# Two attention layers and a two-branch recurrence on one core: the gated branch's level products in column halves, the recurrence's quadrant products trimmed

## What is computed

```
b = jnp.cumsum(lf_c, axis=1)
diff = b[:, :, None] - b[:, None, :]
decay = jnp.where(causal, jnp.exp(jnp.where(causal, diff, 0.0)), 0.0)
att = jnp.einsum('btshd,bshd->btsh', q_c[:, :, None] * decay, k_c)
o_intra = jnp.einsum('btsh,bshv->bthv', att, i_c)
o_inter = jnp.einsum('bthd,bhdv->bthv', q_c * jnp.exp(b), S)
```

## Time and profile before

| | |
|---|---|
| median of 3 runs | 3076.45 us |
| the profiled execution | 3077.23 us, span 3075.4 us |
| TensorE busy | 2974.4 us (97%), 15930 records |
| weight loads | 2378.2 us |
| VectorE busy | 1698.2 us (55%) |
| ScalarE busy | 1210.0 us (39%) |
| mean granted clock of TensorE | 0.988 |

### The profile page before, as it was taken

The page is one execution under the profiler, slowest core; times in us unless marked ns, Lnnn a source line. Parts: engine busy times, 40 slices in busy tenths (PEclk is TensorE's granted clock), DMA queues, the critical chain, the costliest instruction groups (busy, mean ns, idle before and its releaser), DMA issues.

```text
span 3075.4 us, 40378 instructions
## 1 busy us (share of the span) xinstructions
PE 2974.4 (97%) x15930; PEld 2378.2 (77%) x15930; DVE 1698.2 (55%) x2880; ACT 1210.0 (39%) x2131; POOL 284.9 (9%) x517
## 2 busy tenths in 40 slices
PE   9999999999999999999999999999999999999897
PEld 7778787777878877777778877777777877867786
DVE  6554545555553336566553355657566666565647
ACT  5443443434332324344343333434444343434422
POOL 0110101010000000000000002202021020213001
PEclk9999999999999999999999999999999999999899
DMA  4222222222234321222234323223222231225334
GB/s 166 81 77 83 83 77 82 83 83 76 83 124 144 110 89 64 74 69 69 69 108 146 122 82 91 71 62 98 71 83 84 63 105 56 91 74 152 126 130 157
DMA packets 86011, 289.05 MB, mean 94 GB/s; under 512 B 12080, under 2 KB 12720, under 8 KB 85568
## 3 DMA queue, kind: packets, MB, share of 16 engines
q1 hardware_dynamic: 69696, 243.66, 23.4%
q0 software_dynamic: 16128, 42.81, 4.5%
HBM read 261.13 MB, written 25.17 MB: 93 GB/s over the span
## 4 chain that ended last, share of the span: by engine, by line
PE 82%; DVE 10%; ACT 4%; issue 3%; DMA 1%; POOL 0%; DVEq 0%; SPq 0%; ACTq 0%; POOLq 0%
PE bank L280 15%; PE bank L282 14%; PE bank L281 14%; PE bank L284 8%; PE bank L286 7%; PE bank L285 7%; PE bank L1420 2%; DVE mc_split L741 1%; ACT mc_split L573 1%; PE bank L337 1%; PE bank L317 1%; PE bank L1301 1%; PE bank L489 1%; PE bank L476 1%; PE bank L500 1%
## 5 line engine op out<-in xcount | busy, mean ns | idle before, releaser
L280 PE MATMUL bank<-ma_split,mc_split 128*128 128x512 f32 x2304 | 959.1, 416 | 12.1 <-DVE ma_split L895 7.2
L741 DVE TENSOR_TENSOR mc_split<-mc,mc_split 128x1024 fp32r<-128x1024 f32 x434 | 535.2, 1234 | 787.4 <-ACT mc_split L573 786.4
L282 PE MATMUL bank<-ma_split,mc_split 128*128 128x512 f32 x2304 | 906.8, 394 | 0.0
L281 PE MATMUL bank<-ma_split,mc_split 128*128 128x512 f32 x2304 | 904.0, 392 | 0.0
L573 ACT ACTIVATE mc_split<-mc 128x1024 fp32r<-128x1024 f32 x434 | 457.8, 1056 | 656.3 <-PE bank L284 349.4
L280 PEld LDWEIGHTS bank<-ma_split,mc_split 128*128 128x128 f32 x2304 | 437.2, 190 | 122.3 <-issue 48.6
L282 PEld LDWEIGHTS bank<-ma_split,mc_split 128*128 128x128 f32 x2304 | 435.5, 189 | 97.1
L281 PEld LDWEIGHTS bank<-ma_split,mc_split 128*128 128x128 f32 x2304 | 437.8, 190 | 79.0 <-issue 4.4
L284 PE MATMUL bank<-mc_split,ma_split 128*128 128x512 f32 x576 | 230.7, 401 | 5.0 <-DVE mb L1840 3.4
L286 PE MATMUL bank<-mc_split,ma_split 128*128 128x512 f32 x576 | 225.7, 392 | 0.0
L285 PE MATMUL bank<-mc_split,ma_split 128*128 128x512 f32 x576 | 225.2, 391 | 0.0
(11 more groups left out here) (370 smaller groups left out, 3610.9 us busy)
## 6 DMA issues: line engine op xcount, KB each, us to landing
mc<-in_w SPq DMA_DIRECT2D x434, 512.0 KB, 3.2
x<-mc POOLq DMA_DIRECT2D x8, 1024.0 KB, 5.0
y<-mb_split SPq DMA_DIRECT2D x28, 256.0 KB, 2.3
ma_split<-y POOLq DMA_DIRECT2D x28, 256.0 KB, 4.4
mb<-in_xt SPq DMA_DIRECT2D x8, 512.0 KB, 9.3
mc<-in_x POOLq DMA_DIRECT2D x4, 1024.0 KB, 5.4
mc<-x POOLq DMA_DIRECT2D x4, 1024.0 KB, 7.0
mats<-mc POOLq DMA_DIRECT2D x32, 128.0 KB, 2.2
```

Of the source, the lines that this page charges most:

```text
L280: mm = pe.matmul(banks[j][:], wh[:, c], act_hi[:, kt, :], start=(kt == 0), stop=False)
L281: pe.matmul(banks[j][:], wl[:, c], act_hi[:, kt, :], start=False, stop=False)
L282: last = pe.matmul(banks[j][:], wh[:, c], act_lo[:, kt, :], start=False, stop=(kt == KT - 1))
L741: dve.tensor_tensor(w_low[:, s % NR, :, :], w_raw[:, s % NR, :, :], w_high[:, s % NH, :, :].bitcast(F32), ALU.subtract).then_inc(w_lo, 1)
```

## The change

Levels 0 to 5 of a gated head never join tokens of different halves of a chunk. Their products are now made per half: 8 products per level, alternating between key rows 0 to 63 and 64 to 127 of the output, each with at most 64 weight columns and 32 moving columns. The levels are done in pairs at steps 9, 11 and 13, each level of a pair in its own quarter of bank 7; the diagonal is done in halves too, at step 9, in the other half of the bank. Level 6 stays as it was, at step 14. Steps 8, 10, 12 and 15 have no product. VectorE copies each half apart, and for a pair's second level and the diagonal it waits for its own earlier copies. In the recurrence, the second part of levels 4 and 5 loads 48 and 34 weight columns, where it loaded 64 (`half_level_rows`), and the copy takes as many rows.

```diff
-            D_USES |= {("hg", m): 1 for m in (0, *range(8, 16), 17, 24)} | {("hg", m): 1 + (m < 21) for m in range(18, 22)}
+            HG_PAIRS = {9: (0, 1), 11: (2, 3), 13: (4, 5)}
+            HG_DIAG = 9
+            D_USES |= {("hg", m): 4 + 2 * (m == HG_DIAG) for m in HG_PAIRS}
+            D_USES |= {("hg", m): 1 for m in (0, 14, 17, 24)} | {("hg", m): 1 + (m < 21) for m in range(18, 22)}
...
+            def half_level_rows(lv):
+
+                return HD if lv >= LEVELS else HD - (1 << lv) + 2 * (lv == LEVELS - 2)
...
+            def half_cols(x, lv, half):
+
+                n = HD >> (lv + 1)
+                return halves(four(x), lv)[1][:, :, half * n:(half + 1) * n, :]
+
+            def pair_bank(lv, half):
+
+                at = P * (lv % 2)
+                return D_BANK[half_rows(half), at:at + P].rearrange("p (q n t) -> p q n t", q=NCH, t=1 << lv)
+
+            def diag_bank(half):
+                return four(D_BANK[half_rows(half), 2 * P:4 * P])
...
-                            mm = pe.matmul(out, xw[rows, q, half * HD:(half + 1) * HD], in_half(xt, lv, half, 1)[:, q],
+                            n = half_level_rows(lv)
+                            mm = pe.matmul(out[0:n], xw[rows, q, half_rows(half, n)], in_half(xt, lv, half, 1)[:, q],
                                            start=True, stop=True)
...
-                if 8 <= m < 16:
-                    lv = m - 8
...
+                if m in HG_PAIRS:
+                    pe.wait_ge(h_mix, 14 * h + 2 * HG_PAIRS[m][-1] + 2)
+                    for lv in HG_PAIRS[m]:
+                        for c in range(NCH):
+                            for half in range(2):
+                                to, frm = pair_bank(lv, half)[:, c], half_cols(mix[lv % 2], lv, half)[:, c]
+                                n = half_level_rows(lv)
+                                mm = pe.matmul(to[0:n], four(mix[lv % 2])[:, c, half_rows(half, n)], frm, start=True, stop=True)
+                    if m == HG_DIAG:
+                        for c in range(NCH):
+                            for half in range(2):
+                                mm = pe.matmul(diag_bank(half)[:, c], four(hk)[:, c, half_rows(half)],
+                                               four(hqs)[:, c, half_rows(half)], start=True, stop=True)
+                    mm.then_inc(d_done, 1)
...
+                if m in HG_PAIRS:
+                    d_wait(dve, "hg", h, m)
+                    taken = D_BEFORE["hg", h, m]
+                    for lv in HG_PAIRS[m]:
+                        for half in range(2):
+                            n = half_level_rows(lv)
+                            if lv % 2:
+                                dve.wait_ge(d_free, taken + half + 1)
+                            mask = in_half(lmaskt[:, lv:lv + 1, :], lv, half, 1)[0:n]
+                            keep_where(dve, in_half(att, lv, half, 1)[0:n], mask.broadcast_to([n, NCH, *mask.shape[2:]]),
+                                       pair_bank(lv, half)[0:n]).then_inc(d_free, 1)
+                    if m == HG_DIAG:
+                        for half in range(2):
+                            rows = half_rows(half)
+                            dve.wait_ge(d_free, taken + half + 3)
+                            keep_where(dve, att[rows, :, rows], lmaskt[rows, LEVELS:LEVELS + 1, rows].broadcast_to([HD, NCH, HD]), diag_bank(half)).then_inc(d_free, 1)
                 if 7 <= m < 14:
                     level_mix(dve, m - 7, h)
                 if 7 <= m < 12:
                     level_in(dve, m - 5, h)
-                if 8 <= m < 16:
+                if m == 14:
                     d_wait(dve, "hg", h, m)
```

More of the change, by code:

```diff
@@ L1219, in level_rows, with half_rows @@
                 return P if lv >= LEVELS else P - (1 << lv) + 2 * (lv >= FIRST_LEVEL)
-            def half_rows(half):
-                return slice(half * HD, (half + 1) * HD)
+            def half_rows(half, n=HD):
+                return slice(half * HD, half * HD + n)
+            def half_level_rows(lv):
+                return HD if lv >= LEVELS else HD - (1 << lv) + 2 * (lv == LEVELS - 2)
             def in_half(x, lv, half, odd):
@@ L1409, in hg_pe @@
                     turn4(pe, D_BANK, hi_).then_inc(d_done, 1)
-                if 8 <= m < 16:
-                    lv = m - 8
[L1412 to L1417, removed]
+                if m in HG_PAIRS:
[13 more added lines that the diff above has]
+                if m == 14:
+                    lv = LEVELS - 1
+                    rows = level_rows(lv)
+                    pe.wait_ge(h_mix, 14 * h + 2 * lv + 2)
+                    to, frm = halves(four(D_BANK[:]), lv)[1], halves(four(mix[lv % 2]), lv)[1]
                     for c in range(NCH):
-                        rows = level_rows(lv)
-                        mm = pe.matmul(to[0:rows, c], lhs[:, c * P:c * P + rows], frm[:, c], start=True, stop=True)
+                        mm = pe.matmul(to[0:rows, c], mix[lv % 2][:, c * P:c * P + rows], frm[:, c], start=True, stop=True)
                     mm.then_inc(d_done, 1)
@@ L1813, in chunk_dve @@
                         if lv < LEVELS - 1:
-                            mask = in_half(lmaskt[:, lv:lv + 1, :], lv, p, 1)
-                            keep_where(dve, in_half(xt, lv, p, 1), mask.broadcast_to([HD, 2 * NCH, *mask.shape[2:]]),
-                                       half_bank(C_BANK[f"T{lv}{p}"], lv, p)).then_inc(c_dve, 1)
+                            n = half_level_rows(lv)
+                            mask = in_half(lmaskt[:, lv:lv + 1, :], lv, p, 1)[0:n]
+                            keep_where(dve, in_half(xt, lv, p, 1)[0:n], mask.broadcast_to([n, 2 * NCH, *mask.shape[2:]]),
+                                       half_bank(C_BANK[f"T{lv}{p}"], lv, p)[0:n]).then_inc(c_dve, 1)
                         else:
@@ L1892, in hg_dve @@
                     level_in(dve, m - 5, h)
-                if 8 <= m < 16:
+                if m == 14:
                     d_wait(dve, "hg", h, m)
-                    lv, to, frm = m - 8, att, four(D_BANK[:])
-                    if lv < LEVELS:
-                        to, frm = halves(to, lv)[1], halves(frm, lv)[1]
+                    lv = LEVELS - 1
                     rows = slice(0, level_rows(lv))
-                    keep_where(dve, to[rows], level_mask(lv), frm[rows]).then_inc(d_free, 1)
+                    keep_where(dve, halves(att, lv)[1][rows], level_mask(lv), halves(four(D_BANK[:]), lv)[1][rows]
+                               ).then_inc(d_free, 1)
                 if m == 16:
```

## The result

The changed kernel took 3093.02 us (median of 4 runs, 3090.44 to 3094.05), the kernel before 3076.14 us in the same session (4 runs, 3072.79 to 3076.53). The ratio is 1.0056, 95% interval 1.0044 to 1.0068: slower by 17 us, where I had forecast 15 us faster. The profiled execution took 3094.05 us (span 3092.2); its mean granted clock is 0.986, against 0.988.

What follows compares the result with a forecast made beforehand. TensorE, busy for 97% of the span, was taken to bound the kernel. Halves -14.8, trim -4.2, (a) -7.4, (b) +5, (c) +2, (d) +4 sum to -15.4 us: 3061 us, range 3048 to 3074.

Steps and rivals of the forecast that it cites:

- What TensorE's work costs: TensorE's queue: column halves of levels 0 to 5 and the diagonal gain 14.8 us, the recurrence's trimmed products 4.2 us.
- Rival 3: Gated branch: the halves' weight loads take turns, a pair costs 0.11 us, the run takes 3083 us; chance 0.07.
- rival 4: TensorE: no pair under 0.058 us, trim brings nothing, groups 11 and 13 stay at 1.30; 3068 us; chance 0.12.
- Step (a): Bank 7: the diagonal's claim behind the block's end (4.7 us) and level 1's (1.2 us) go; gain 7.4 us.
- Step (b): Blocks' ends: VectorE's four copies before level 6's inputs at step 13 delay the take; 5 us back, bounds 0 and 9.
- Step (c): Group 11: level 3's inputs behind six copies (2.1 us) just fit; 1 us, plus 1 us for recurrence steps.
- nine places: Between TensorE's groups, first six heads: nine places of 0.69 us, into which level 3's late inputs just fit.
- Step (d): Last two heads: the 7.4 us wait moves to group 9, with new waits before later groups; cost 4 us.
- the 1.5 that I had counted as a gain: First head: lower granted clock behind the longest wait cost about 1.5 us, counted within Step (a)'s gain.
- Rival 2: VectorE takes most of the gain: up to 9 us at blocks' ends, more in later groups; 3071 us; chance 0.13.
- The range: Run time: 3048 to 3074 us, leaving out Rival 3 and the ends of two other rivals.

Runs made afterwards that it cites:

- single levels: The kernel before with levels 0 to 5 and the diagonal in halves at their old steps, one copy per level; 3066.15 us, ratio 0.9968.
- The other experiment with an early diagonal: The changed kernel with inputs ahead of copies and the diagonal taken from step 9's group to step 7, one copy; 3059.96 us, ratio 0.9948.
- turning the order: The changed kernel, but at steps 9, 11 and 13 VectorE makes the next levels' inputs before the copies; 3066.9 us, ratio 0.997.
- The better version: The kernel before with halves at old steps, one copy per level, the trim, and the diagonal moved from step 15 to 7; 3056.23 us, ratio 0.9933.
- the wide pairs: The changed kernel with full-width products in its pairs, one copy per level, the diagonal back at step 15; 3104.43 us, ratio 1.0095.

## Why the prediction was wrong

**What TensorE's work costs** was right, to 0.1 us a group. The halves gained 16.5 us where I had 14.8, the trim 4.9 us by its rows (3.6 us when run alone) where I had 4.2. Rival 3 and rival 4 are out: the group of step 11 takes 1.17 us, not over 1.7, and 34 columns go faster than 48. The Trainium skill (TensorE: Matmul & The Clock Gate, Part 3, "The mechanism"), read strictly, has the halves' loads take turns because they use one row group; the trace doesn't agree, at 32 moving columns either: 24 pairs in 1.72 us are 0.07 us a pair with the group's ends included. The floor of 25 ns from start to start that the same page of the Trainium skill states ("Wait, 56ns, not 53.3ns?") isn't borne out either: 32 records (16 pairs) in 0.72 us are less than 23 ns each.

**Step (a)**, the diagonal's and level 1's claims on bank 7, was right: no wait of a diagonal product is left among after's waits, and with single levels the early diagonal gave about 7 us, where I had 7.4. The other experiment with an early diagonal, also about 7 us, is no evidence for it: these claims were gone there already, and what it took away is two of the six copies behind step 9. What (a) overlooked is the new claim of 1.7 us before L1304.

**Step (b)**, the take held up at the blocks' ends, had the right sign and mechanism: 4.6 us against 1.7 us, so 2.9 us, where I took 5. In the first head the first product behind it starts at 2007.89 us after 1.32 us idle, as the 1.4 us had it.

**Step (c)** failed: "this just fits in the first six heads; I allow 1 us, and 1 us more for recurrence steps that find VectorE later". It is the mis-sized term. In the first six heads the level groups waited 7.0 us, where I allowed 1 (three of the five waits are of 1.9 to 2.3 us, before step 11), and the recurrence's steps waited 17.9 us more, where I allowed 1; turning the order gave 25.7 us of the span back. Three things in it were wrong. The six copies take 2.82 us, 0.47 us each, not 2.1; the 0.34 us came from level 5's copy, and those of levels 0 and 1 take longer (last section). I counted what stands between the wait and the inputs on VectorE's queue and not what those late inputs hold up on ScalarE: its exponential, the weight split behind it, VectorE's split behind that, and only then level 3's operands. That link left VectorE idle for 1.65 us at this place. And I gave the slack of "nine places" to TensorE's group alone, while every step of the recurrence in the same stretch also draws on VectorE. ScalarE's part wasn't isolated: an order with its split ahead of the exponential wasn't run. And 9.7 us of the recurrence's waits stay when the order is turned; that they go with the pairs is shown (with single levels 1.3 to 2.0 us are left), by which copies is not.

**Step (d)** was right for the last head and short for the one before. TensorE's level groups in the last head:

```profile
2895.64 1.92 PE L1438 MATMUL bank<-mb 128*63 128x32 f32 x32 [8.37 <-DVE mb L1891]
...
2906.67 1.04 PE L1438 MATMUL bank<-mb 128*60 128x32 f32 x32 [2.49 <-DVE mb L1891]
...
2912.35 0.82 PE L1438 MATMUL bank<-mb 128*48 128x32 f32 x32 [1.70 <-DVE mb L1891]
...
2915.54 0.66 PE L1451 MATMUL bank<-mb 128*66 128x64 f32 x8 [0.79 <-DVE mb L1891]
```

The wait moved to group 9 as said, and behind it stand 2.49, 1.70 and 0.79 us, where I had 1.9, 1.8 and 0.7. Head 6, which I took to come out even, waited 2.7 us before step 13. With the rest of group 9's, (d)'s waits are 8.8 us and not 4.4.

**The two sums.** From my -15.4 to the span's +16.8 are 32.2 us: (c) 22.9, (d) 4.8 (rounded terms), the clock 5.0 and the 1.5 that I had counted as a gain, less 2.1 of (b) and 2.4 of products: 29.7. The other 2.5 are in small waits that I did not follow.

**Rival 2** named the right engine and three of the places, with 3071 us. It allowed "3 us more in groups 11 and 13" and nothing for the recurrence. No rival of mine ended slower by VectorE; the one that did (rival 3) had the wrong engine.

**The range** failed with (c). Its bounds were drawn from TensorE's side, which had been measured, and (c) had a value but no bounds of its own: no row showed six copies ahead of an input, and the nearest rows (a copy 0.44 us, a split 1.22 us behind it, ScalarE idle) would have given an upper end of several us per head.

The better version keeps what was right: 3056 us, by the medians about half from the halves in before's own order, a third from the early diagonal, the rest from the trim.

## What to carry over

Where an engine copies another's product out and also makes the inputs of a later product, the inputs go ahead of the copies, and of the wait where the buffers allow it; put behind them, they must be followed through every in-order queue that they feed, down to the instruction that the bottleneck waits for. A wait on TensorE can also cost the slower clock behind it, in the changed kernel about a seventh on top (5.0 us for 32.4). That is no fixed rate: the wide pairs had 21.4 us more of waits and 26 slow steps, one fewer than before. When work is gathered into fewer, larger groups, price the burst of copies behind each group at its measured length and bound that term from both sides, even where the engine is busy for only 55% of the time.

## What the runs showed of the hardware

- Two products that share all 128 rows and write different column halves run in pairs. The 16 pairs of 63 and 62 weight columns in group 9 take 1984.59 - 1983.66 = 0.93 us, 0.058 us for a pair of records, where one record of a full-width product of level 0 takes 0.88 / 8 = 0.11 us. A group of 16 pairs costs 1.17 us at 60 and 56 weight columns and 0.95 us at 48 and 34: the time follows the weight columns down to 34, with no floor in sight.
- Splitting a level in halves gains about 0.1 us on its own (0.85 to 0.75 us). The rest of the changed kernel's gain comes from gathering: the seven sets of halves cost 5.12 us one by one and 3.84 us in three groups, (5.12 - 3.84) / 4 = 0.32 us for each group saved. It is tempting to call that the price of a switch between large and small products, but the wide pairs rule it out: two full-width levels in one group cost 1.77 us, the same as apart. So a group of halves has a fixed price of about 0.3 us that a full-width group has not. No run here shows why.
- Halving a copy's elements hardly shortens it. The six copies behind step 9 (63 x 128, 62 x 128 and 64 x 256 elements, two of each) took 0.47 us each from start to start, and the four behind step 13 (48 x 128 and 34 x 128) 0.32 us each, where a whole level of 98 x 256 lets the next instruction start after 0.34 us. In the kernel before, levels 1 and 2 copy almost the same number of elements (behind the first bar: busy us in all, mean ns of one):

```profile
L1243 DVE COPY_PREDICATED mb<-lmaskt,bank 126x256 f32<-126x256 uint8 x8 | 5.9, 733 | 3.6 <-PE bank L1420 3.6
...
L1243 DVE COPY_PREDICATED mb<-lmaskt,bank 124x256 f32<-124x256 uint8 x8 | 3.5, 436 | 2.5 <-PE bank L1420 2.4
```

The first, with runs of 2 tokens, takes 0.73 us, as level 0's with single tokens does; the second, with runs of 4, takes 0.44 us, as level 5's with runs of 32 does. So it is the length of the runs that counts, and between 2 and 4.
